# Second block's attention: the first rows' probabilities are turned by VectorE's block transposes instead of TensorE

## What is computed

```python
def swa_sink_attention(q, k, v, sinks, band_bias, band_mask):
...
    s = jnp.einsum('bnqkgd,bnskd->bnkgqs', q, kb).astype(jnp.float32) * (ATT_HEAD_DIM ** -0.5)
    s = jnp.where(band_mask[None, :, None, None], s + band_bias, NEG)
    m = jnp.maximum(jnp.max(s, axis=-1, keepdims=True), sink)
    e = jnp.exp(s - m)
    p = e / (jnp.sum(e, axis=-1, keepdims=True) + jnp.exp(sink - m))
    o = jnp.einsum('bnkgqs,bnskd->bnqkgd', p.astype(v.dtype), vb)
```

## Time and profile before

| | us |
|---|---|
| median of 3 runs | 2441.27 (2441.05 to 2442.01) |
| the profiled execution, its own time | 2440.69 |
| its span, first to last instruction | 2438.9 |
| TensorE busy | 2430.3 |
| VectorE busy | 1935.7 |
| ScalarE busy | 1262.9 |
| GpSimd busy | 105.5 |

### The profile page before, as it was taken

How to read it: one execution, slowest core, us unless ns; L and a number is a source line. 1 busy time by engine, 2 the same in 40 slices (tenths; PEclk the granted TensorE clock), 3 DMA queues, 4 the chain that set the end, 5 groups by cost and what they waited for, 6 DMA issues and landing times.

```text
span 2438.9 us, 30567 instructions
## 1 busy us (share of the span) xinstructions
PE 2430.3 (100%) x11718; PEld 2023.7 (83%) x11718; DVE 1935.7 (79%) x3077; ACT 1262.9 (52%) x1678; POOL 105.5 (4%) x128
## 2 busy tenths in 40 slices
PE   9999999999999999999999999999999999999999
PEld 7888888888888888888888888888888888888887
DVE  8777978878878788888767798877877867797876
ACT  5445654454456544544556655544544557664543
POOL 0000000000000000000100020000000100020000
PEclk9999999999999999999999999999999999999999
DMA  7775456656754566676554564555666644555663
GB/s 257 237 236 174 156 189 190 192 188 194 238 181 155 174 196 200 202 231 212 175 195 141 172 217 156 189 196 183 206 194 201 199 163 153 171 204 169 198 195 121
DMA packets 325904, 463.34 MB, mean 190 GB/s; under 512 B 18608, under 2 KB 237056, under 8 KB 325504
## 3 DMA queue, kind: packets, MB, share of 16 engines
q1 hardware_dynamic: 321792, 452.90, 57.3%
q10 hardware_dynamic: 3968, 8.49, 1.1%
HBM read 457.11 MB, written 4.23 MB: 189 GB/s over the span
## 4 chain that ended last, share of the span: by engine, by line
PE 99%; DMA 0%; DVE 0%; ACT 0%; SPq 0%; DVEq 0%; issue 0%; ACTq 0%
PE acc L712 48%; PE work L712 39%; PE acc L880 4%; PE acc L883 2%; PE work L935 1%; PE acc L972 1%; PE work L719 1%; PE work L953 1%; PE work L747 1%; PE acc L1214 0%; PE work L1124 0%; PE acc L1213 0%; PE acc L747 0%; DMA raw<-ffn_w_dram 0%; PE work L1009 0%; PE work L1202 0%
## 5 line engine op out<-in xcount | busy, mean ns | idle before, releaser
L1781 DVE TENSOR_TENSOR w_lo<-raw,w_hi 128x2048 fp32r<-128x2048 f32 x416 | 948.0, 2284 | 239.6 <-ACT w_hi L1261 236.6
L1261 ACT CAST w_hi<-raw 128x2048 fp32r<-128x2048 f32 x416 | 788.5, 1902 | 282.3 <-PE work L712 102.0
L712 PE MATMUL work<-w_hi,xt_both 128*128 128x512 f32 x2816 | 882.5, 389 | 0.9 <-DVE xt_both L1812 0.6
L712 PEld LDWEIGHTS work<-w_hi,xt_both 128*128 128x128 f32 x2816 | 528.5, 188 | 111.7 <-DVE w_lo L1788 1.5
L712 PE MATMUL work<-w_lo,xt_both 128*128 128x512 f32 x1408 | 547.8, 389 | 0.0
L712 PE MATMUL acc<-w_hi,yt_hi 128*128 128x512 f32 x1088 | 428.3, 394 | 0.0
L712 PE MATMUL acc<-w_hi,yt_lo 128*128 128x512 f32 x1088 | 423.9, 390 | 0.0
L712 PE MATMUL acc<-w_lo,yt_hi 128*128 128x512 f32 x1088 | 423.4, 389 | 0.0
L1950 DVE STREAM_TRANSPOSE field<-field 32x128 f32<-32x128 f32 x1280 | 387.7, 303 | 19.1
L712 PE MATMUL acc<-w_hi,xt_both 128*128 128x512 f32 (+2 forms) x1280 | 394.4, 384 | 0.0
L712 PEld LDWEIGHTS work<-w_lo,xt_both 128*128 128x128 f32 x1408 | 264.3, 188 | 54.6
(11 more groups left out here) (201 smaller groups left out, 1554.7 us busy)
## 6 DMA issues: line engine op xcount, KB each, us to landing
raw<-ffn_w_dram SPq DMA_DIRECT2D x260, 512.0 KB, 4.6
raw<-w_in_dram SPq DMA_DIRECT2D x208, 512.0 KB, 4.5
raw<-w_ffn_in_dram SPq DMA_DIRECT2D x176, 512.0 KB, 4.6
raw<-w_ffn_out_dram SPq DMA_DIRECT2D x88, 512.0 KB, 4.2
raw<-w_branch_dram SPq DMA_DIRECT2D x48, 512.0 KB, 4.4
raw<-w_out_dram SPq DMA_DIRECT2D x32, 512.0 KB, 4.4
bias<-b_gate_dram SPq DMA_DIRECT2D x10, 512.0 KB, 5.5
raw<-w_branch_pool_dram SPq DMA_DIRECT2D x8, 512.0 KB, 4.2
```

The source lines that it names most:

```text
L712: last = nc.tensor.matmul(out, x[:, kt, k], y, start=start and n == 0, stop=stop and n == 2)
L1261: nc.scalar.copy(w_hi[:, slot, 0:n], raw[:, at, 0:n]).then_inc(hi_split[slot], 1)
L1781: nc.vector.tensor_tensor(w_lo[:, at, 0:n], raw[:, at, 0:n], w_hi[:, slot, 0:n].bitcast(F32), ALU.subtract).then_inc(unit_split[slot], 1)
```

## The change

Of both groups' first rows, in both layers of the second block, the turn of the probabilities goes from TensorE to VectorE. VectorE's transpose turns blocks of 32x32, so a 128x128 tile is four times four of them; one instruction takes the same block of four or eight tiles. `turn_early(g, part)` writes the turned tiles into places of `field` that are free by then (`early_t`). The first group is done in two halves of four tiles each, `turn_early(0, 0)` before the retention product and `turn_early(0, 1)` behind `mask(0, 1)`; the second group's eight tiles at once, behind `through(27)`. The last instruction of a group signals `early_turned[g]`, and `values` waits for it. TensorE's `turn_probs(0, 0)` and `turn_probs(1, 0)`, ScalarE's `copy_probs` for them and their rows in `WORK` are gone.

```diff
-    [("rowsA", 1), ("decay", 4), ("kT", 1), ("scores00", 4), ("ret", 4), ("probsT00", 4), ("scores01", 4), ("turn_r", 4),
-     ("probsT01", 4), ("scores10", 4), ("scores11", 4), ("probsT10", 4), ("probsT11", 4),
+    [("rowsA", 1), ("decay", 4), ("kT", 1), ("scores00", 4), ("ret", 4), ("scores01", 4), ("turn_r", 4),
+     ("probsT01", 4), ("scores10", 4), ("scores11", 4), ("probsT11", 4),
...
+        early_t = lambda g, hp: view((7168 if g else 8192) + 256 * hp, 2, P)
...
+                early = block and not r and g in (0, 1)
                 if not block and not r:
                     pe.wait_ge(probs_turned_low, l + 1)
+                if early:
+                    pe.wait_ge(early_turned[g], l + 1)
...
                 chunk("rg", 1, 16)
-                turn_probs(0, 0)
                 both("gate_r", 0, 0, 18)
...
                 both("gate_a0", 0, 0, 26)
-                turn_probs(1, 0)
                 both("gate_a0", 0, 1, 26)
...
                 rows("rg", 1, 17, R["g"], ACT.Silu)
-                copy_probs(1, l, 0, 0, B["e"])
...
                 through(29)
-                copy_probs(1, l, 1, 0, B["e"])
...
+                def turn_early(g, part=None):
+
+                    dve.wait_ge(probs_scaled, events(1, l, [8 * n for n in PASSES], 8 * g + 4))
+                    places = ((4096, 7168, 8),) if g else ((512, 8192, 4), (1536, 8704, 4))
+                    for src, dst, n in places if part is None else places[part:part + 1]:
+                        for o in range(4):
+                            for i in range(4):
+                                last = nc.vector.transpose(view(dst, n, P)[32 * o:32 * o + 32, :, 32 * i:32 * i + 32],
+                                                           view(src, n, P)[32 * i:32 * i + 32, :, 32 * o:32 * o + 32])
+                    if part != 0:
+                        last.then_inc(early_turned[g], 1)
...
                 through(19)
+                turn_early(0, 0)
                 for c in range(2):
                     pair, n = chunk_count(1, l, "rg", c)
...
                 through(20)
                 mask(0, 1)
+                turn_early(0, 1)
                 through(21)
...
                 mask(1, 1)
+                through(27)
+                turn_early(1)
                 through(28)
```

More of the change, by code:

```diff
@@ L277, in build @@
         low_taken = sem("low_taken")
+        early_turned = [sem(f"early_turned{g}") for g in range(2)]
         qk_turned = sem("qk_turned")
@@ L961, in values @@
                 pe.wait_ge(chunk_read[pair], n * 2)
+                early = block and not r and g in (0, 1)
                 if not block and not r:
                     pe.wait_ge(probs_turned_low, l + 1)
+                if early:
+                    pe.wait_ge(early_turned[g], l + 1)
                 for i in range(0, 4, 2):
                     for s in range(2):
-                        if block or r:
+                        if r or block and not early:
                             turned(block, l, f"probsT{g}{r}", i + s)
@@ L970, in values @@
                             for s in range(2):
-                                pT = (e(g, r, i + s) if block or r else probs_t(i + s)).rearrange("p s n -> p (s n)")
+                                pT = (early_t(g, i + s) if early else e(g, r, i + s) if block or r else probs_t(i + s)) \
+                                    .rearrange("p s n -> p (s n)")
                                 last = nc.tensor.matmul(
```

## The result

The changed kernel takes 2455.6 us (median of 6 runs, 2453.64 to 2455.9), the kernel before 2441.34 us (6 runs beside them, 2441.0 to 2442.5): 1.0057 times as long, interval 1.0047 to 1.0067. The time lies in the forecast range, but where the first rival had put it and not where the forecast case had. The profiled execution took 2453.64 us with a span of 2451.8, 12.9 us more than before. It is the shortest of the six.

The account below looks back on a forecast made before the run. TensorE's stream was taken to bound the kernel. Net of removed transposes, 4.45 + 1.0 us a layer gave +11.0 us on 2440.69, 2451.7, and 0.6 for the median gave 2452.3 us; range 2449.5 to 2458.

Parts of the forecast that it names:

- the first rival: At the two long pauses before gather(0,0): TensorE's clock falls, +3 to +6 us, 2455 to 2458 us; chance 0.36.
- the forecast case: Whole kernel: late VectorE queue makes TensorE wait before both gathers; 2452.3 us, range 2449.5 to 2454, chance 0.54.
- That TensorE's stream bounds the kernel: Whole span: TensorE holds 99% of the chain, so every microsecond taken from its stream shortens the kernel.
- what its transposes are worth: Four places on TensorE, two groups in two layers: removal saves 0.87 us each, 3.5 us in all.
- The batches: VectorE, per layer: two half batches of 5.08 us and one of 7.2 us, total 17.3 us.
- The walk down the queue: VectorE's order: add_bias 6.6 us late, gather(0,0) at 1316.3; TensorE waits 5.3 us there, 1.7 us before gather(1,0).
- The terms of the sum: Per layer: 4.45 us for the first group plus 1.0 us for the second; 11.0 us over two layers.
- What is late next: ScalarE's two tanh on gate_r 0 end near 1317.0, 3.8 us late, yet in time for the later TensorE.
- The clock falls: TensorE restarts at 1.2 GHz after the 5.3 us pauses before gather(0,0): +3 to +6 us in two layers; chance 0.36.
- The working from the opening of the program: First 48 matmuls take 93 ns each against 62 ns later, so a cold start costs 1.5 us.
- The rival on the other side: At the add_bias before gather(0,0): batches stay hidden, only the saving is left, 2437.8 us; chance 0.04.
- The limit it names: Before gather(0,0): at 2.16 us a half batch, 0.135 us a transpose, TensorE waits 0.87 us and the group is even.

Follow-up runs that it names:

- experiment 10: Kernel before with both groups' first-row turn left out on every engine (not computed rightly): 2438.14 us, ratio 0.9986.
- experiment 5: Kernel before, TensorE's transposes kept, with VectorE's three batches added on constants and nothing waiting for them: 2454.99 us, ratio 1.0056.
- experiment 8: Changed kernel with the first group's second half batch moved behind the next split and add_bias of gate_r 0: 2455.2 us, ratio 1.0058.
- experiment 6: Changed kernel without 8 of the 16 transposes of the first group's second half (not computed rightly): 2447.41 us, ratio 1.0024.
- experiment 3: Changed kernel with 80 small unused matmuls on TensorE before the wait of gather(0,0): 2451.5 us, ratio 1.0041.
- experiment 9: Changed kernel with 8 of 16 transposes of the first group's first half and none of its second (not computed rightly): 2440.91 us, ratio 0.9998.
- experiment 4: Changed kernel without the 16 transposes of the first group's second half, early_turned still signalled (not computed rightly): 2443.82 us, ratio 1.0009.

## Why the prediction was right or wrong

**That TensorE's stream bounds the kernel, and what its transposes are worth.** Right: 0.87 us a place forecast, 0.82 measured (experiment 10).

**The batches.** Right: 5.05 and 5.04 us for the half batches, and the large one 7.18 us, as in the earlier trace rows; the strides cost nothing. The Trainium skill (VectorE: DVE Perf Modes, "The three transpose paths") lists 311 ns for a bf16 tile on VectorE and 390 ns on TensorE; its "Rules for kernel authors" nevertheless send a 128x128 transpose to TensorE where its result may go to PSUM. The runs side with the rule and not with the order of the two figures: eight fp32 tiles cost TensorE's stream 0.82 us (experiment 10) and VectorE 7.18 us.

**The walk down the queue.** Right to 0.3 us. Start of the mask 1301.4 forecast, 1301.21 measured; second half batch 1307.6 and 1307.33; split 1312.7 and 1312.40; `gather(0, 0)` 1316.3 and 1316.07. Pauses 5.3 forecast and 5.02 measured, 1.7 and 1.67. The releaser was the `add_bias`, as said; experiment 5 shows that it is the queue and not the data, experiment 6 that it is one to one, experiment 8 that in the other order the mark `early_turned` is late by as much.

**The terms of the sum.** Slightly too large: 4.45 us for the first group where 4.22 and 4.13 came, 1.0 for the second where 0.9 came. I had counted several starts in VectorE's queue from the end of the instruction before, but most successors start some hundredths early (the split at 1299.01, before L2295 ends at 1299.08). 10.1 us in place of 11.0; experiment 3 has 10.0 with the clock held up.

**What is late next.** Right: ScalarE's tanh moved with the `add_bias` (they end at 1316.68, forecast near 1317.0) and TensorE didn't wait for it. In the changed kernel TensorE's longest wait besides the four pauses and the one of the earlier trace rows is 0.5 us.

**The clock: the step that failed.** "The clock falls" was a rival with 0.36, and the forecast case left the clock at 1.00. It fell in both layers. The price in the rival, 3 to 6 us for both together, was right: 3.2 us in the profiled execution, 4.1 us in the median by experiment 3. The sum of 2452.3 us is 0.8 us above experiment 3, where the clock is held up, and 3.3 us short of the result. The forecast case's own range ended at 2454 us; the stated range holds the result only because it was drawn to cover this rival. The working from the opening of the program gave the right size (1.5 us a fall; 1.85, 1.34 and 1.6 us came), but the record doesn't show that it is the same thing: the granted clock over the opening's 48 matmuls (1.36 to 5.84 us) stands at 1.00. The error was how I weighed the evidence: that no row of before shows a fall said nothing, because no row of before has a pause of more than 1.4 us either. The pauses that the forecast itself made were of a new kind, and I treated the absence of rows as if it spoke for the old behaviour. The Trainium skill (TensorE: Matmul & The Clock Gate, "Why this matters for your kernels"), which advises against letting TensorE pause between bursts, was quoted and given too little weight; the trace agrees with it (a 5.02 us pause, and a granted clock of 0.72 over the 12 us around it).

**The rival on the other side.** It didn't come about; the batches had their 5.05 us. The limit it names, 2.16 us for a half batch, wasn't tried as such; the nearest is experiment 9, where a first batch of 2.50 us and no second lost nothing. But the walk looks at the `add_bias` alone. Experiment 4, with 5.05 us in the first half and nothing in the second, had the `add_bias` in time for TensorE and still took 2.5 us more than that alone would give, by the late mask and the banks of `turn_probs(0, 1)`. Two chains hang behind the first half batch, and I had followed one.

## What to carry to other kernels

Before moving work to a helper that is 79% busy, find which release stands behind the place in the helper's queue and how much slack it has (2.16 us here, and 3.65 us of idle in the queue ahead of it, against 10 us of new work). Walk every chain that hangs behind the place, not only the nearest. If the work is worth moving, cut it to the length of the idle stretches, use the largest instruction, and move the consumer back in the bounding engine's order: together these turned +14 us into -2.8. And when a forecast contains a pause of the bounding engine longer than any in the trace, its clock afterwards belongs in the sum and not in a side case.

## What the runs showed of the hardware

- Around two pauses of 5.0 us the granted clock was lower (0.72 and 0.86 over 12 us, for 1.85 and 1.34 us of loss); around two of 2.49 us once lower and once not, in one and the same execution; around pauses of 1.67 us it stayed at 1.00. The fall isn't tied to the pause's end: it came after 2.1 us of one 5.0 us pause, after 4.5 us of the other, and 0.7 us behind the end of a 2.49 us one. The same pause can thus cost 1.6 us or nothing, which also fits the spread of experiment 6's runs (2445.67 to 2447.98). Why two equal pauses differ stays open.
- 80 small bf16 matmuls in the pause (58 ns each) kept the clock up, and paid 4.1 us.
- A block transpose of VectorE has a large part that doesn't grow with its size: 16 of 32x128 take 5.05 us, 16 of 32x256, twice the data, 7.18 us. Per 128x128 fp32 tile that is 1.26 us and 0.90 us. An estimate from these two: 0.18 us of the 0.32 us of a small one is fixed.
